# Expert layer of a two-layer decoder: gather of picked rows against a dense pass over the whole expert table

## The reference, cut to what matters

```
# xb: (288, 1024) normalised tokens; eu, ev: (16384, 1024)
q = (xb @ wq).reshape(n, 8, 2, 128)
s1 = einsum('nhd,kd->nhk', q[:, :, 0], k1)      # 128 scores
s2 = einsum('nhd,kd->nhk', q[:, :, 1], k2)      # 128 scores
t1, i1 = top_k(s1, 16);  t2, i2 = top_k(s2, 16)
ts, ti = top_k(t1[..., :, None] + t2[..., None, :], 16)   # of 256
e = i1[ti // 16] * 128 + i2[ti % 16]            # 16 experts a head
g = softmax(ts)
hid = gelu(einsum('nd,nhkd->nhk', xb, eu[e]))
y = einsum('nhk,nhkd->nd', g * hid, ev[e])
```

## Time and profile before

| What | Value |
|---|---|
| Median of three runs | 1822.72 us |
| Span of the profiled execution | 1820.2 us |
| Time minus span, about | 2.5 us |
| TensorE busy | 1551.5 us (85%) |
| VectorE busy | 1110.6 us (61%) |
| ScalarE busy | 605.4 us (33%) |
| GpSimd busy | 701.3 us (39%) |
| Granted TensorE clock, mean | 0.954 |
| Traffic over DMA | 730.03 MB, mean 401 GB/s |

### The profile page before, as it was taken

The page is one execution under the profiler, slowest core; times in us unless marked ns, Lnnn a source line. Parts: engine busy times, 40 slices in busy tenths (PEclk is TensorE's granted clock), DMA queues, the critical chain, the costliest instruction groups (busy, mean ns, idle before and its releaser), DMA issues.

```text
span 1820.2 us, 18420 instructions
## 1 busy us (share of the span) xinstructions
PE 1551.5 (85%) x5782; PEld 831.6 (46%) x5782; DVE 1110.6 (61%) x2783; ACT 605.4 (33%) x1873; POOL 701.3 (39%) x682
## 2 busy tenths in 40 slices
PE   8999997999888877788689999979888887877777
PEld 5779644554343332233147895545443333322221
DVE  3445766566888774444535367574868878654444
ACT  2332432333344332222333334323334423322222
POOL 5111343455544443334413024534464444434341
PEclk9999999999898899899999999989999988999999
DMA  9899999899999999999979989999999999999997
GB/s 334 319 386 355 410 412 421 365 421 422 420 421 421 422 421 422 421 423 420 422 295 396 379 355 407 420 374 416 421 422 420 422 421 422 421 421 421 421 423 309
DMA packets 102838, 730.03 MB, mean 401 GB/s; under 512 B 14993, under 2 KB 16114, under 8 KB 21972
## 3 DMA queue, kind: packets, MB, share of 16 engines
q0 software_dynamic: 90432, 627.75, 83.6%
q1 hardware_dynamic: 11760, 100.48, 13.9%
q10 hardware_dynamic: 548, 0.62, 0.1%
HBM read 724.54 MB, written 48.10 MB: 424 GB/s over the span
## 4 chain that ended last, share of the span: by engine, by line
PE 42%; DMA 41%; DVE 10%; ACT 3%; issue 2%; DVEq 1%; ACTq 1%; POOL 0%; SPq 0%
DMA arena<-peer_uv,idx 24%; PE bank L1762 22%; DMA wring<-peer_uv,idx 8%; PE bank L1518 7%; PE bank L1686 5%; DVE arena L1340 3%; DMA qf<-peer_uv,idx 3%; PE bank L1726 2%; DMA yt<-peer_uv,idx 2%; DMA wring<-w_out 2%; DMA arena<-peer_wq 2%; DVE wring L1340 1%; PE bank L1513 1%; ACT diag L864 1%; DVE yt L1340 1%
## 5 line engine op out<-in xcount | busy, mean ns | idle before, releaser
L1762 PE MATMUL bank<-arena,diag 128*128 128x512 f32 (+1 forms) x1416 | 679.2, 623 | 109.4 <-ACT diag L864 109.3
L1340 DVE SCALAR_TENSOR_TENSOR arena<-arena,xn 128x1024 f32<-128x1024 f32 x378 | 458.4, 1225 | 330.0 <-DMA arena<-peer_uv,idx 326.4
L641 POOL DMA_INDIRECT arena<-peer_uv,idx x378 | 410.0, 1085 | 617.9 <-PE bank L1762 462.8
L1762 PEld LDWEIGHTS bank<-arena,diag 128*128 128x128 f32 (+1 forms) x1416 | 265.3, 193 | 476.1 <-issue 298.5
L856 ACT ACTIVATE act<-hid 128x2 f32<-128x2 f32 x287 | 58.4, 204 | 903.4 <-DVE arena L1340 594.1
L864 ACT ACTIVATE diag<-ident,weight 128x128 f32<-128x128 f32 (+1 forms) x574 | 194.3, 385 | 20.9 <-issue 1.4
L1762 PE MATMUL bank<-wring,diag 128*128 128x512 f32 x336 | 165.2, 631 | 37.2 <-ACT diag L864 37.1
L641 POOL DMA_INDIRECT wring<-peer_uv,idx x84 | 98.8, 1176 | 129.0 <-PE bank L1762 119.9
L1762 PE MATMUL bank<-qf,diag 128*128 128x512 f32 (+1 forms) x216 | 111.3, 655 | 40.9 <-ACT diag L864 40.9
L1340 DVE SCALAR_TENSOR_TENSOR wring<-wring,xn 128x1024 f32<-128x1024 f32 x84 | 102.3, 1225 | 69.7 <-DMA wring<-peer_uv,idx 68.4
L859 ACT ACTIVATE weight<-act,gate 128x1 f32<-128x1 f32 x574 | 138.0, 287 | 19.8
(11 more groups left out here) (290 smaller groups left out, 1564.9 us busy)
## 6 DMA issues: line engine op xcount, KB each, us to landing
kvs<-cache_a_kv_w SPq DMA_DIRECT2D x32, 1022.0 KB, 10.7
wring<-w_col SPq DMA_DIRECT2D x15, 1024.0 KB, 8.1
wring<-w_tok SPq DMA_DIRECT2D x8, 1408.0 KB, 9.0
arena<-peer_wq SPq DMA_DIRECT2D x10, 1024.0 KB, 18.1
kvs<-cache_a_kv_w SPq DMA_DIRECT2D x16, 508.0 KB, 11.9
arena<-peer_uv,idx POOLq DMA_INDIRECT x378
qf<-cache_keys POOLq DMA_DIRECT2D x8, 576.0 KB, 10.7
qf<-cache_values POOLq DMA_DIRECT2D x8, 576.0 KB, 19.1
```

The costliest lines, as they stand in the source:

```text
L641: pool.indirect_dma_start(out=ring[j], out_offset=None, in_=io["peer_uv"], in_offset=bass.IndirectOffsetOnAxis(ap=idx[:, n:n + 1], axis=0) ...
L1340: last = v.scalar_tensor_tensor(out=ring[j][:, 0:D], in0=ring[j][:, 0:D], scalar=1.0, in1=xn[:, i, :], op0=ALU.mult, op1=ALU.mult, accum_o ...
L1762: last = pe.matmul(bank[b0 + half][0:r, :], diag[:, n % 16, 0:r], ring[SLOT_OF[n]][:, D + 512 * half:D + 512 * half + 512], start=False, s ...
```

## The change

The gather goes. The u table is laid out beforehand in 128 blocks, one for each value of the second key i2; a block is 128 partitions of features by 8 chunks of 128 first keys i1, 512 KB. The v table too has 128 blocks, of i1 by 1024 features. In the up phase every block is multiplied with all 288 tokens (`up`: 8 calls with 128x128 weights and 288 columns), and ScalarE writes gelu of the result to `hw`, a buffer of 128 x 288 values a partition. In the down phase every block of `hw` is multiplied with the v block (`down`: 7 calls of 288 columns and one output chunk split in 160 and 128 columns, because eight chunks share seven banks), accumulated in PSUM over all 128 blocks.

In between, `hw` is multiplied by the gates. For each token, VectorE builds two one-hot matrices over its 128 picks: first key times gate, 128 x 128 (`tensor_scalar`), and second key, 128 x 64 for one half of the keys (`tensor_tensor`). TensorE multiplies them to that token's gate matrix (`gates`: 8 calls of 64 columns for 8 tokens), and VectorE multiplies `hw` by it from PSUM (`scale`). There are 36 passes of 8 tokens for each of the two halves; the first half goes in the second part of the up phase, the second half in the first part of the down phase.

The result comes out with features on partitions, so the turns between layouts (`turn_x`, `token_rows`, `open_y`) go, and the next layer's norm is over the whole width (`x_add`, `x_square`, `x_mean`, `x_root`, `x_scale`, `norm_apply`) after the last down block. All queries are now computed before the first up block, all routing runs beside the up phase, and no projection of the next layer is brought forward. The cache copies move out of the front into the block loops, in pieces of 16 rows.

```diff
-PARTS = ((0, 0, 1), (0, 1, 1), (0, 2, 2), (0, 4, 2), (0, 6, 2), (1, 0, 2), (1, 2, 2), (1, 4, 2), (1, 6, 2), (2, 0, 2))
+PARTS = ((0, 0, 2), (0, 2, 2), (0, 4, 2), (0, 6, 2), (1, 0, 2), (1, 2, 2), (1, 4, 2), (1, 6, 2), (2, 0, 2))
...
+HALF = NK // 2
+TG = 8
+PASS = TOKENS // TG
+U_SLOTS, V_SLOTS = 4, 6
+SCORE_BEHIND = {3: 0, 4: 2, 5: 4, 6: 7, 7: 13, 8: 21}
+COPY_BEFORE = {3: 1, 4: 4, 5: 9, 6: 17, 7: 25, 8: 33}
+EXP_BEFORE = {0: 0, 1: 7, 2: 15, 3: 23, 4: 31, 5: 38, 6: 46, 7: 54, 8: 62}
+TURN_BEHIND = {0: 30, 1: 60, 2: 68}
+PASS_BEHIND = [g * 60 // PASS for g in range(PASS)]
...
-                    pool.indirect_dma_start(
-                        out=ring[j], out_offset=None, in_=io["peer_uv"],
-                        in_offset=bass.IndirectOffsetOnAxis(ap=idx[:, n:n + 1], axis=0)).then_inc(row_in[j], 16)
...
+            def load_u(l, n):
+                s, _ = slot_loads(l, 0, n)
+                if n < U_SLOTS:
+                    sp.wait_ge(qf_ps, NQ * l + q_count(1 + n // 2, 1, REST))
+                else:
+                    sp.wait_ge(block_used, used(l, 0, n - U_SLOTS + 1))
+                sp.dma_start(slot[s], io["u_blocks"][l, n]).then_inc(block_in[s], 16)
...
+                for n in range(NK):
+                    load_u(l, n)
+                    if n >= 8:
+                        shift(l, n - 8)
+                for n in range(NK):
+                    load_v(l, n)
...
+            def gelu(l, n):
+                a.wait_ge(block_used, used(l, 0, n + 1))
+                a.activation(hw[:, n, :], bank[n % 3][:, 0:TOKENS], ACT.Gelu_apprx_tanh).then_inc(gelu_done, 1)
...
-            def dots(l, b):
...
-                    last = v.scalar_tensor_tensor(out=ring[j][:, 0:D], in0=ring[j][:, 0:D], scalar=1.0, in1=xn[:, i, :],
-                                                  op0=ALU.mult, op1=ALU.mult, accum_out=hid[:, n:n + 1])
...
+            def one_hots(l, g):
+                n0, hf = g % PASS * TG, g // PASS
+                if g % PASS == 0 or n0 in T0:
+                    v.wait_ge(turned, TILES * (l + 1) if hf else TILES * l + T0.index(n0) + 1)
+                if g > 1:
+                    v.wait_ge(pass_ps, 2 * PASS * l + g - 1)
+                for t in range(TG):
+                    v.tensor_scalar(hot_a[g % 2][:, t, :], count[:, :], picks[:, 0, n0 + t:n0 + t + 1], picks[:, 2, n0 + t:n0 + t + 1],
+                                    ALU.is_equal, ALU.mult)
+                v.tensor_tensor(hot_b[g % 2], count[:, HALF * hf:HALF * hf + HALF].unsqueeze(1).broadcast_to([P, TG, HALF]),
+                                picks[:, 1, n0:n0 + TG].unsqueeze(2).broadcast_to([P, TG, HALF]), ALU.is_equal).then_inc(hot_done, 1)
+            def scale(l, g):
+                n0, hf = g % PASS * TG, g // PASS
+                v.wait_ge(pass_ps, 2 * PASS * l + g + 1)
+                if g % PASS == 0:
+                    v.wait_ge(gelu_done, NK * l + HALF * (hf + 1))
+                h = hw[:, HALF * hf:HALF * hf + HALF, n0:n0 + TG]
+                v.tensor_tensor(h, h, pass_bank(g)[:, :].rearrange("p (t j) -> p j t", t=TG), ALU.mult).then_inc(scaled, 1)
...
+                for g in range(2 * PASS):
+                    one_hots(l, g)
+                    if g:
+                        scale(l, g - 1)
+                scale(l, 2 * PASS - 1)
+                for n in range(KCH):
+                    x_add(l, n)
...
-            def add_rows(l, n, i, last_one):
...
-                    last = pe.matmul(bank[b0 + half][0:r, :], diag[:, n % 16, 0:r], ring[SLOT_OF[n]][:, D + 512 * half:D + 512 * half + 512],
-                                     start=False, stop=last_one)
...
+            def gates(l, g):
+                pe.wait_ge(hot_done, 2 * PASS * l + g + 1)
+                behind = g - (1 if g >= PASS else 2)
+                if behind >= 0:
+                    pe.wait_ge(scaled, 2 * PASS * l + behind + 1)
+                for t in range(TG):
+                    last = pe.matmul(pass_bank(g)[:, t * HALF:(t + 1) * HALF], hot_a[g % 2][:, t, :], hot_b[g % 2][:, t, :], start=True, stop=True)
+                last.then_inc(pass_ps, 1)
+            def up(l, n):
...
+                if n > 2:
+                    pe.wait_ge(gelu_done, NK * l + n - 2)
+                pe.wait_ge(block_in[s], target)
                 for k in range(KCH):
+                    last = pe.matmul(bank[n % 3][:, 0:TOKENS], slot[s][:, k * P:(k + 1) * P], xt[:, k, :], start=(k == 0), stop=(k == KCH - 1))
+                last.then_inc(block_used, 1)
+            def down(l, n):
...
+                pe.wait_ge(block_in[s], target)
+                for k in ACC_ORDER:
+                    for acc_ps, c in acc_of(k):
+                        last = pe.matmul(acc_ps, slot[s][:, k * P:(k + 1) * P], hw[:, n, c],
+                                         start=(n == 0 and k not in (3, 4)), stop=(n == NK - 1 and k < KCH - 1))
...
+                for q in range(2, NQ):
+                    queries(l, q)
...
+                for n in range(NK):
+                    up(l, n)
...
+                    for g in range(PASS):
+                        if HALF + PASS_BEHIND[g] == n:
+                            gates(l, g)
+                for n in range(NK):
+                    down(l, n)
+                    for g in range(PASS):
+                        if PASS_BEHIND[g] == n:
+                            gates(l, PASS + g)
```

More of the change, by code:

```diff
@@ L102 @@
+Q_ORDER += [(c, j, WHOLE) for c in range(4, 8) for j in range(2)]
+NQ = len(Q_ORDER)
 PITCH = 384
 LOW = -3.0e38
[L105 to L130, removed]
@@ L281, in take @@
             at += n
-            return arena[:, at - n:at]
+            return big[:, at - n:at]
+        hw = big[:, :].rearrange("p (j n) -> p j n", j=NK)
+        flat_w = take(2 * W_SLOT)
+        wring = flat_w.rearrange("p (s n) -> p s n", s=2)
+        flat_xn = take(TILES * D)
+        flat_yt = take(KCH * TOKENS)
+        yt = flat_yt.rearrange("p (k n) -> p k n", k=KCH)
+        keys_at = at
+        kc = [take(9 * P).rearrange("p (c n) -> p c n", c=9) for _ in range(5)]
+        at = HALF * TOKENS
+        wmt = take(CH * P).rearrange("p (h n) -> p h n", h=CH)
+        gcv = take(CW)
+        mixb = take(3 * P).rearrange("p (c n) -> p c n", c=3)
+        ktt = take(2 * NK).rearrange("p (s n) -> p s n", s=2)
+        at = 20480
+        arena_at = at
         raw = take(6 * TOKENS).rearrange("p (j n) -> p j n", j=6)
@@ L646, in _, with used, slot_loads @@
+        def used(l, phase, n):
+            return (2 * NK - 1) * l + NK * phase + n
+        def slot_loads(l, phase, n):
+            s = n % (V_SLOTS if phase else U_SLOTS)
+            a_layer = [(NK // U_SLOTS if s < U_SLOTS else 0), len(range(s, NK, V_SLOTS))]
+            before = sum(a_layer) * l + (a_layer[0] if phase else 0)
+            return s, 16 * (before + n // (V_SLOTS if phase else U_SLOTS) + 1)
+        block = ctx.enter_context(nc.Block())
         @block.scalar
@@ L820, in h_root @@
                 a.wait_ge(hms_ps, 2 * l + part + 1)
[L821 to L830 removed]
+                a.activation(rs[:, c], hms_of(c), ACT.Sqrt, bias=eps[:, 0:1]).then_inc(hroot_done, 1)
             def qf_copy(l, q):
@@ L992, in _ @@
-            y_last()
+                h_root(l, 1)
+                for q in range(2, NQ):
+                    qf_copy(l, q)
+                    if q in (5, 9, 21):
+                        score_copy(l, (5, 9, 21).index(q))
+                for n in range(NK):
+                    for p in range(NP):
+                        if COPY_BEFORE.get(p) == n:
+                            score_copy(l, p)
+                        if EXP_BEFORE[p] == n:
+                            gate_exp(l, p)
+                    for i in range(TILES):
+                        if TURN_BEHIND[i] + 2 == n:
+                            picks_copy(l, i)
+                    gelu(l, n)
@@ L1041, in norm_apply, with x_add, x_scale @@
                 last.then_inc(xt_done, 1)
+            def x_add(l, n):
+                k = ADD_ORDER[n]
+                v.wait_ge(y_ps, KCH * l + max(ACC_ORDER.index(k) + 1, 3 if k == KCH - 1 else 0))
+                for acc_ps, c in acc_of(k):
+                    last = v.tensor_tensor(xr[:, k, c], acc_ps, xr[:, k, c], ALU.add)
+                last.then_inc(x_done, 1)
+            def x_scale(l):
+                v.wait_ge(xroot_done, l)
+                v.reciprocal(rs[:, :], rs[:, :])
+                v.drain()
             def cv_means(l, n, tiles):
```

1087 lines of the change are left out of this document (404 added, 683 removed).

## The result

The changed kernel takes 2732.63 us (median of four runs, 2732.21 to 2732.85) against 1823.55 us before (four runs): 1.50 times as long, 95% interval 1.497 to 1.503. The forecast was 2732, likeliest case "as summed". The profiled execution took 2732.21 us with a span of 2730.5; the sum had 2730. Time minus span is thus 1.7 us here, not the 2.5 that was added.

A forecast was written before the change was run, and what follows sets the result against it. The kernel before was taken as bound by the gather's transfers. On TensorE in one line, 137 + 2 x (104 + 1128.5) + 120 + 8 = 2730 us of span gave 2732 us of time, range 2690 to 2870.

The forecast's parts named there:

- as summed: Whole kernel: the likeliest case, all terms added with no rival striking, 2732 us, within 2700 to 2800; chance 0.82.
- What bounds the kernel before: Gather stage of the kernel before: bound by its transfers, about 740 us a layer, 1480 of 1820.
- The price of a call: TensorE matmuls: a 288-column float32 call with fresh 128x128 weights is two records, 0.485 us.
- Up stage: Up phase, a layer: 128 blocks of 8 calls at 0.485, 496.6 us, before gates, scores, turns and gap.
- Down stage: Down phase, a layer: 128 blocks at 3.89 us, 498.0 us, before its gates.
- Covers: Block stages: VectorE, ScalarE, block loads and cache copies stay hidden behind TensorE; a pass 3.5 us against 8.2.
- VectorE's pass: Gates: 3.5 us a pass; the rival has VectorE set the pace from 8.2, 2990 us at 10; chance 0.05.
- Fronts: Work before each layer's first output projection: 137 us in layer 0, 120 in layer 1 including its transition.
- Traffic: DMA, whole kernel: near 375 MB (730 - 628 + 268), DMA share near a third in the block stretches.
- the lower clock: Unbroken float32 matmuls: rival that only 0.95 clock is granted, adding 118 us, 2850 us; chance 0.05.
- Blocks landed: Block loads: rival that they land late, deciding from 11.6 us; 2820 us at 13, 3140 at 18.1; chance 0.04.
- The one on the other side: Table and gate calls: rival that a call costs one record's distance, halving 2238 us, time 1613 us; chance 0.01.

The follow-up runs named there:

- before_half: The kernel before, each gathered row 4 KB instead of 8, with the same number of calls, dots and hand-overs: 1559.48 us, 0.857 of before.
- high_both: The kernel after, with `up` and `down` operands read in place as bfloat16 upper halves of the float32 words: 1441.93 us, 0.792 of before.
- no_gates: The kernel after without gates, one-hots and scaling, so `hw` is not multiplied: 2475.47 us.
- gates_128: The kernel after, with seven of the eight gate calls of a burst writing 128 columns in place of 64: 2731.44 us.
- hot_x2: The kernel after, with VectorE writing the first-key one-hots two times, a drain between: 2734.09 us.
- hot_x4: The kernel after, with VectorE writing the first-key one-hots four times, with drains between: 2960.55 us.
- high_hots: The kernel after with bfloat16 upper halves in `up` and `down`, and one-hots also written and multiplied as bfloat16: 1363.67 us, 0.749 of before.

## Why the prediction was right, point by point

- **What bounds the kernel before** (the bytes of the gather): right, shown by before_half.
- **The price of a call**, 0.485 us with 288 columns as two records: right within 1%. The stream without bursts has 242.4 ns a record, as the earlier trace rows gave. That the price belongs to the float32 type is shown by high_both.
- **Up stage**, 496.6 + 8 + 62.2 + 1.5 = 568.3 us: 570.1. **Down stage**, 498 + 62.2 = 560.2: 562.3 and 562.4. Both 2 us short: a burst costs some 0.05 us beyond its records, 36 times a stage, that I had taken as nothing (no_gates: 1.786 a pass in place of 1.728). The gap between the phases was 0.50 us, not 1.5; the scores and turns were 102 records, not some 70, and took about the 8 us all the same. The 50 us that I had held open for block changes without bursts did not appear.
- **Gates** at 108 ns a record: right, and that the columns don't count is shown (gates_128).
- **Covers**: VectorE's pass 3.5 us as summed, though its terms were 2.13, 0.68 and 0.69 in place of 2.30, 0.64 and 0.55; hidden up to 5.7 at least (hot_x2); blocks in 3.3 us against 11.6; SyncE, ScalarE and the cache copies on no path.
- **Projection and queries**, 104: 101.0 twice. The sum of the calls, 101, was exact and the 3 us for small waits were not needed; TensorE has no idle time in either window.
- **Fronts**: first output projection 137: 138.1. Front of layer 1 with its transition 120: 121.4. The transition itself was 8.9 us: the last block's matmuls end the stage at 1371.6, and the first projection starts at 1380.50 behind 4.84 us of idle time on the last scaled chunk, the one wait of TensorE near there:

```profile
1371.61 4.04 PE L1350 MATMUL bank<-big,means 128*128 128x288 f32 x16
1380.50 3.72 PE L1375 MATMUL bank<-big,xt 128*128 128x352 f32 x7 [4.84 <-DVE xt L930]
```

- **End**, 8: 4.0 (2726.5 to 2730.5). I doubled the old end without a row for it; it stayed the same. Time minus span, 2.5: 1.7.
- **Traffic**, 375 MB: 395.56, on no path. The terms given for it add up to 370, and one is wrong: the first queue's 628 MB are not all gather. The 576 columns of 128 rows of 8 KB are 604 MB; the other 24 stay in the kernel after, whose first queue moves 24.33 MB. 730 - 604 + 268 is 394. The DMA share of the block stages was 0.37 to 0.42, where a third was forecast.

The errors have both signs: +1.1 us in the first front, -6 in the queries of both layers, +7.9 in the four block stages, +1.4 in the second front, -4 at the end. They cancel to 0.5, and that closeness is partly luck; that each block stage lies within some 2 us, the queries within 3 and the end within 4, is not.

Of the rivals, the lower clock did not appear (1.00 in every block stage). Blocks landed in 3.3 us where trouble starts at 11.6, and VectorE's pass took 3.5 where it starts at 8.2. The one on the other side, one record's price a call, needs another operand type: then the kernel ends at 1442 us. That is below the 1613 that halving gave, since a call falls to 128 ns and not to 242, and far above the 1030 of one pass for everything, because the gates keep their price and transfers and routing come up behind.

## What to carry to other kernels

A dense pass in place of a gather trades bytes for matmul columns, so price both in the type that the kernel really uses: here 485 ns a float32 call against 128 ns a bfloat16 call decides between 1.50 times slower and 0.79 of before, with the same bytes moved and the same waits. When a stage will be one unbroken stream of one engine, the distance between starts in the trace of before, times the count, is the forecast; spend the care on checking the covers against their turning points. And when a price falls by a factor, look up who stands next before counting the gain: a DMA at 0.4, a VectorE at 0.43 or less and an 8.2 us slot for a 3.5 us pass were all but used up at once. Not tried: one pass of gates for both halves of the keys, which gates_128 suggests would save up to half of the 257 us, but which needs all gates before the first down block.

## What the runs showed of the hardware

- Every second bfloat16 value of a buffer (the upper halves of float32 words) can be both operands of a matmul at 128 ns for 288 columns (high_both), with nothing converted or copied beforehand.
- A wait of TensorE can cost it more than its length. In hot_x4 behind 3.96 us of idle time the 16 gate records took 3.14 us in place of 1.73, and the 32 block records 9.84 in place of 7.81: 3.4 us on top of 4. The granted clock was 1.00 before (560 to 567.5 us), and 0.74 over these 13 us, a mean of the two levels, 1.2 and 2.4 GHz. Not every wait does it, and not the longer ones alone: behind 1.35 us of idle time (597.24) the next records ran at 0.85, behind 3.01 us (626.95) at 1.00. Windows of hot_x4, each from the end of such a wait on:

```profile
567.50:580.50 13.00, 12.97 (x48) 10.59 (x49) 12.69 (x45) 0.41 (x1) 0.00 (x0) 0.74 0.15 50
...
597.20:608.50 11.30, 11.26 (x48) 9.20 (x49) 11.06 (x39) 0.41 (x1) 0.00 (x0) 0.85 0.30 111
...
626.95:636.86 9.91, 9.82 (x49) 7.80 (x49) 9.68 (x35) 0.47 (x2) 0.00 (x0) 1.00 0.20 66
```

- The narrow type hardly helps VectorE in these shapes (high_hots): eight `tensor_scalar` of 128x128 take 1.88 us as bfloat16 against 2.13, and `tensor_tensor` of 128x512 0.69 in both.
- Four block stages of 562 to 570 us of unbroken float32 matmuls were granted a clock of 1.00; the kernel before, which waited, had 0.954 over its span.
